# Sample cross-attention on four 32-column quarters of TensorE, two heads at a time

## What is computed

```
def cross_attend(h, mem_k, mem_v, w_q, w_o):          # 4 heads of 256, 256 memory tokens
    q = (h @ w_q).reshape(b, L, XA_HEADS, XA_HEAD_DIM)
    s = jnp.einsum('blhd,bmhd->bhlm', q, mem_k) * (XA_HEAD_DIM ** -0.5)
    p = jax.nn.softmax(s, axis=-1)
    o = jnp.einsum('bhlm,bmhd->blhd', p, mem_v).reshape(b, L, D_MODEL)
    return o @ w_o
```

## Time and profile before

| | |
|---|---|
| median of 3 runs | 1892.45 us (1890.16 to 1892.65) |
| the profiled execution, device time | 1889.55 us |
| its span, first to last instruction | 1887.5 us |
| TensorE busy in the span | 1793.5 us (95%) |
| VectorE / ScalarE / GpSimd busy | 506.8 / 300.8 / 31.9 us |
| read from memory | 356.67 MB, 202 GB/s over the span |

### The profile page before, as it was taken

How to read it: one execution, slowest core, us unless ns; L and a number is a source line. 1 busy time by engine, 2 the same in 40 slices (tenths; PEclk the granted TensorE clock), 3 DMA queues, 4 the chain that set the end, 5 groups by cost and what they waited for, 6 DMA issues and landing times.

```text
span 1887.5 us, 18695 instructions
## 1 busy us (share of the span) xinstructions
PE 1793.5 (95%) x7908; PEld 1127.3 (60%) x7908; DVE 506.8 (27%) x1066; ACT 300.8 (16%) x666; POOL 31.9 (2%) x34
## 2 busy tenths in 40 slices
PE   7999999999999899999899999999999998999996
PEld 5776676577666654444367666766667666544442
DVE  0027653441110311121200185534211013111122
ACT  2114220130120210001111142102211102100101
POOL 0000000000100000000000000000010000000000
PEclk9999999799999799999999999999999997999998
DMA  6323215553264279999813322255423551999992
GB/s 270 129 94 134 93 45 200 201 200 134 89 223 178 90 280 391 356 386 369 357 61 118 139 88 90 94 200 219 178 90 134 214 187 58 400 361 390 360 386 122
DMA packets 28681, 382.68 MB, mean 203 GB/s; under 512 B 3184, under 2 KB 3568, under 8 KB 3888
## 3 DMA queue, kind: packets, MB, share of 16 engines
q1 hardware_dynamic: 25040, 356.69, 48.9%
q0 software_dynamic: 3552, 24.71, 3.2%
HBM read 356.67 MB, written 24.71 MB: 202 GB/s over the span
## 4 chain that ended last, share of the span: by engine, by line
PE 87%; DVE 4%; ACT 4%; DVEq 2%; issue 1%; DMA 1%; ACTq 0%; POOL 0%; SPq 0%; POOLq 0%
PE psum L472 29%; PE psum L925 12%; PE psum L750 7%; PE psum L945 6%; PE psum L910 5%; PE psum L970 4%; PE psum L809 3%; PE psum L839 3%; PE psum L713 2%; PE psum L690 2%; PE psum L710 2%; DVE work L1455 2%; PE psum L700 2%; PE psum L479 1%; PE psum L877 1%
## 5 line engine op out<-in xcount | busy, mean ns | idle before, releaser
L472 PE MATMUL psum<-h,ring 128*128 128x320 f32 x1920 | 533.7, 438 | 7.7 <-DVE h L1380 6.3
L472 PEld LDWEIGHTS psum<-h,ring 128*128 128x128 f32 x1920 | 366.8, 192 | 164.9 <-issue 17.3
L925 PE MATMUL psum<-ring,work 128*64 128x512 f32 x1024 | 231.9, 597 | 1.6 <-ACT work L1325 1.4
L925 PEld LDWEIGHTS psum<-ring,work 128*64 128x64 f32 x1024 | 69.6, 137 | 137.3 <-issue 132.5
L750 PE MATMUL psum<-work,ring 128*128 128x320 f32 x512 | 138.3, 433 | 0.9 <-ACT work L1100 0.9
L472 PE MATMUL psum<-mem,ring 128*128 128x256 f32 x512 | 123.0, 395 | 4.0 <-ACT work L1100 4.0
L750 PEld LDWEIGHTS psum<-work,ring 128*128 128x128 f32 x512 | 97.1, 190 | 42.0 <-ACT work L1100 1.8
L945 PE MATMUL psum<-ring,work 128*64 128x512 f32 x512 | 115.1, 603 | 7.2 <-ACT work L1340 7.2
L472 PEld LDWEIGHTS psum<-mem,ring 128*128 128x128 f32 x512 | 98.5, 197 | 21.2 <-issue 7.1
L910 PEld LDWEIGHTS psum<-work 128*128 128x128 f32 x768 | 92.1, 199 | 25.0 <-issue 22.7
L910 PE MATMUL psum<-work 128*128 128x128 f32 x768 | 97.8, 286 | 1.4 <-ACT work L1313 1.4
(11 more groups left out here) (242 smaller groups left out, 1467.0 us busy)
## 6 DMA issues: line engine op xcount, KB each, us to landing
ring<-stream SPq DMA_DIRECT2D x168, 2048.0 KB, 9.1
st_out<-states_out POOLq DMA_DIRECT2D x18, 1024.0 KB, 9.2
mk_out<-k_mem POOLq DMA_DIRECT2D x2, 1024.0 KB, 6.1
mv_out<-work POOLq DMA_DIRECT2D x2, 1024.0 KB, 5.6
cst<-consts SPq DMA_DIRECT2D x1, 1456.0 KB, 22.3
x<-x_in SPq DMA_DIRECT2D x1, 1280.0 KB, 5.7
y_out<-h POOLq DMA_DIRECT2D x2, 640.0 KB, 3.2
mem<-mem_in SPq DMA_DIRECT2D x1, 1024.0 KB, 24.2
```

The costliest lines, as they stand in the source:

```text
L472: mm = pe.matmul(out, w[:, a:a + P], rhs[:, j, :], start=(j == 0), stop=(j == KD - 1))
L925: mm = pe.matmul(psum[ab * CAP:(ab + 1) * CAP, up, :], h_packed[:, p % 2, k, ab * CAP:(ab + 1) * CAP], w[:, a:a + BANK], start=(k == 0), s ...
```

## The change

The samples' matmuls use four quarters of the array, 32 columns each. In a group of four requests, request b has stationary columns of its own (its 8 tokens, no zeros), writes rows 32b to 32b+7 of PSUM, and four consecutive matmuls of the source go to four different quarters. The count stays at 64 matmuls for the scores and 64 for the outputs, each with 256 moving columns. `q_own`, `prob_own`, their zeroing on GpSimd and the waits for it are gone; the zero blocks' copies become plain ones (`q_all` takes a chunk in one copy).

Each sample group of four requests is now a tile of 128 rows with 32 used, so there are 4 tiles (`XT`: two of the prompt, two of samples) in place of 2 and a half, each processed for two heads at a time (`hp`). Transposes of probabilities: 32 per layer (24 before); of outputs: 16 (8 before). The transposed probabilities and transposed sample outputs leave PSUM by VectorE instead of ScalarE. Queries are computed in two halves, each followed by the scores of its two heads, and the quads are put in the order MQ0, K0, K1, MQ1, K2, K3, V0 to V3, MO0, MO1; a K or V quad holds four requests and two heads.

The layout constants, and then TensorE's list:

```diff
-Q_MQ = 24
-Q_KC, Q_VC = 26, 30
+Q_MQ = [24, 27]
+Q_KC, Q_VC = [25, 26, 28, 29], [30, 31, 32, 33]
+GB = DB // 4
+XT = 2 + GB
...
+                def queries(hp):
+                    for c in range(4 * hp, 4 * hp + 4):
+                        w = quad(pe, L, Q_MQ[hp])
+                        if c >= 4:
+                            pe.wait_ge(s_qout, L * KD + c - 3)
+                        products(psum[:, 4 + c % 4, 0:T], w, (c % 4) * SLAB, P, h,
+                                 L * NNORM + 1 if c == 0 else None).then_inc(s_q, 1)
+                    free(Q_MQ[hp])
+                def scores(hp):
+                    pe.wait_ge(s_qout, L * KD + 4 * hp + 4)
+                    for t in range(2):
...
+                    for gb in range(GB):
+                        q = Q_KC[2 * hp + gb]
+                        w = quad(pe, L, q)
+                        if hp == 1:
+                            pe.wait_ge(s_xexp, L * 8 + 2 + gb + 1)
+                        for rr in range(2):
+                            for c in range(2):
+                                k = 2 * (2 * hp + rr) + c
+                                for b in range(4):
+                                    own = SEQ + (4 * gb + b) * DS
+                                    a = ((b * 2 + rr) * 2 + c) * M
+                                    mm = pe.matmul(psum[32 * b:32 * b + DS, 2 + gb, rr * M:(rr + 1) * M],
+                                                   q_all[:, k, own:own + DS], w[:, a:a + M],
+                                                   start=(c == 0), stop=(c == 1))
+                                    if rr + c + b == 0:
+                                        first(mm)
+                        mm.then_inc(s_xs, 1)
+                        free(q)
+                def turn_probs(hp):
+                    for i in range(XT):
+                        u = 4 * hp + i
+                        pe.wait_ge(s_prob, L * 8 + u + 1)
+                        if hp == 0:
+                            pe.wait_ge(s_qout, L * KD + 4 + i + 1)
+                        else:
+                            pe.wait_ge(s_xoout, L * KD + i + 1)
+                        for rc in range(4):
...
+                def prompt_out(hp):
+                    for j in range(4 * hp, 4 * hp + 4):
+                        pe.wait_ge(s_ptout, L * 8 + 4 * hp + max(2, j % 4 + 1))
...
+                def sample_out(hp):
+                    pe.wait_ge(s_ptout, L * 8 + 4 * hp + 4)
+                    for gb in range(GB):
+                        q = Q_VC[2 * hp + gb]
+                        w = quad(pe, L, q)
+                        pe.wait_ge(s_xexp, L * 8 + 4 + 2 * hp + gb + 1)
+                        for rr in range(2):
+                            for c in range(2):
+                                for b in range(4):
+                                    own = SEQ + gb * P + 32 * b
+                                    a = ((b * 2 + c) * 2 + rr) * DV
+                                    mm = pe.matmul(psum[32 * b:32 * b + DS, 2 * hp + gb, rr * DV:(rr + 1) * DV],
+                                                   prob_t[:, 2 * hp + rr, c, own:own + DS], w[:, a:a + DV],
+                                                   start=(c == 0), stop=(c == 1))
+                                    if rr + c + b == 0:
+                                        first(mm)
+                        mm.then_inc(s_xos, 1)
+                        free(q)
+                def turn_out(hp):
+                    for gb in range(GB):
+                        pe.wait_ge(s_otok, L * 4 + 2 * hp + gb + 1)
+                        transposes([(psum[:, 2 * hp + gb, i * P:(i + 1) * P],
+                                     o_tok[:, gb, (4 * hp + i) * P:(4 * hp + i + 1) * P])
+                                    for i in range(4)]).then_inc(s_ott, 1)
+                queries(0)
+                scores(0)
+                queries(1)
+                scores(1)
+                turn_probs(0)
+                prompt_out(0)
+                sample_out(0)
+                turn_probs(1)
+                sample_out(1)
+                prompt_out(1)
+                turn_out(0)
+                turn_out(1)
+                pe.wait_ge(s_xoout, (L + 1) * KD)
+                pe.wait_ge(s_ottout, (L + 1) * 4)
```

ScalarE's order is queries(0), exps(0), queries(1), exps(1), prompt_out(0), sample_out(0), sample_out(1), prompt_out(1). VectorE's list, and what goes on GpSimd:

```diff
+                maxima(0)
+                probabilities(0)
+                maxima(1)
+                turned_probs(0)
+                probabilities(1)
+                turned_probs(1)
+                turned_out(0)
+                turned_out(1)
...
-                pool.wait_ge(s_wout, L * 16 + KD)
-                pool.memset(q_own[:], 0.0).then_inc(s_qzero, 1)
-                pool.wait_ge(s_mvstore, 16 * (L + 1))
-                pool.wait_ge(s_vt, (L + 1) * 4)
-                pool.memset(prob_own[:], 0.0).then_inc(s_pzero, 1)
```

More of the change, by code:

```diff
@@ L804, in attention @@
[L804 to L832, removed]
@@ L1259, in exps, with queries @@
[L1259 to L1266, removed]
+                def queries(hp):
+                    for c in range(4 * hp, 4 * hp + 4):
+                        act.wait_ge(s_q, L * KD + c + 1)
+                        act.activation(q_all[:, c, :], psum[:, 4 + c % 4, 0:T], ACT.Copy).then_inc(s_qout, 1)
@@ new lines, in prompt_out, with sample_out @@
+                def prompt_out(hp):
+                    for j in range(4 * hp, 4 * hp + 4):
+                        act.wait_ge(s_xo, L * KD + j + 1)
+                        act.activation(h[:, j, 0:SEQ], psum[:, 4 + j % 4, 0:SEQ], ACT.Copy).then_inc(s_xoout, 1)
+                def sample_out(hp):
+                    for gb in range(GB):
+                        act.wait_ge(s_xos, L * 4 + 2 * hp + gb + 1)
+                        act.activation(o_tok[:, gb, hp * BANK:(hp + 1) * BANK], psum[:, 2 * hp + gb, :], ACT.Copy)\
+                            .then_inc(s_otok, 1)
@@ L1708, in attention, with maxima @@
[L1708 to L1711 removed]
+                def maxima(hp):
+                    for i in range(XT):
+                        u = 4 * hp + i
+                        dve.wait_ge(s_xs, L * 8 + u + 1)
+                        dve.tensor_reduce(xmax[:, u, :], psum[:, i, :].rearrange("p (b m) -> p b m", b=2), AX.X, ALU.max)
+                        dve.drain()
+                        dve.tensor_scalar(xmax[:, u, :], xmax[:, u, :], -1.0 / 16, None, ALU.mult).then_inc(s_xmax, 1)
@@ new lines, in probabilities @@
+                def probabilities(hp):
+                    for i in range(XT):
+                        u = 4 * hp + i
+                        dve.wait_ge(s_xexp, L * 8 + u + 1)
+                        dve.reciprocal(xsum[:, u, :], xsum[:, u, :])
+                        dve.drain()
+                        pr = prob[:, i, 2 * hp:2 * hp + 2, :]
+                        dve.tensor_tensor(pr, pr, xsum[:, u, :].unsqueeze(2).broadcast_to([P, 2, M]), ALU.mult)\
+                            .then_inc(s_prob, 1)
```

167 lines of the change are left out of this document (58 added, 109 removed).

## The result

Median **1830.6 us** (4 runs, 1828.41 to 1838.72), before 1891.31 us beside it: ratio 0.9694, 95% interval 0.9656 to 0.9731, faster by 61 us where 71 were forecast. Later, beside another set of runs of the kernel before, the same kernel gave 0.9667 (0.9643 to 0.9690). Two executions further down, one of e5 (3089.9 us) and one of e6 (3520.7 us), were in a slow state that no edit explains, and all ratios and the medians of e5 and e6 leave them out.

The account below looks back on a forecast made before the run. TensorE, busy 95% of the span, was taken to bound the kernel. Cross-attention savings of 35.4 and 35.2 us, 70.6 in all, took 1889.55 to 1818.9; the median's 2.9 us offset gave 1821.8, range 1811 to 1845.

Parts of the forecast that it names:

- The mechanism: Sample matmuls: four quarters work through their own record lines side by side, 1.9 us a quad, 41 us a layer less before waits.
- the schedule: Hand timeline of one layer's cross-attention, from first query matmul to output projection: 78.0 us; 88.1 with two abreast, 116 with one.
- The 2.2 us a quad: Sample matmuls: a measured three-tile packing, 2.38 times, scaled to four as 3.2 times; sum some 3 us higher over both layers.
- One reading in the prediction: Sample matmuls, argument for the partly-abreast rival: eight records and eight loads must start in every 219 ns.
- the pitch of 55 ns: Sample matmuls: one record starting every 55 ns at the lower bound of 1.75 us a quad.
- the third, the waits: Cross-attention, part 3: new waits, worked out in a one-layer schedule; 35.4 and 35.2 us less per layer, 70.6 in all.
- VC3 late: Second sample outputs: the last V quad lands at about 69.7 us, so TensorE waits 2.1 us.
- The clock rival: Low clock after waits: 20 us of TensorE work up to twice as long, +10 to +15 us a layer, about 1845; chance 0.07.
- MQ1 late: Second half of the queries: the second query-weight quad lands at 27.3 us, so TensorE waits 0.5 us.
- the first four chunks: First half of the queries: with the copy of the fourth chunk, the scores start at 19.3 us.
- The pace behind one another: Quad loads: a lone quad lands 7.7 us after issue; behind another it takes 5.6 us more.
- VectorE's waits: Prompt and sample outputs: TensorE waits for VectorE's copies, 0.7 us before the first prompt outputs and 0.9 before later sample outputs.

Follow-up runs that it names:

- e5: Changed kernel with the first four query chunks in PSUM banks 0 to 3 and the prompt's V-copy wait behind the queries: 1831.3 us, ratio 0.9688.
- e6: Changed kernel with all 8 query chunks first, then the scores of both head pairs, quads reordered to match: 1826.2 us, ratio 0.9671.
- e1: Changed kernel with all sample matmuls on one quarter, leaving out three requests' outputs in four: 1896.0 us, ratio 1.0036 to the kernel before.
- e2: Changed kernel with requests alternating between two quarters, leaving out two requests' outputs in four: 1846.2 us, ratio 0.9763 to the kernel before.
- e4: Changed kernel with the last V quad, VC3, loaded early into a free part of the work area: 1810.8 us, ratio 0.9593.
- e8: Changed kernel with VC3 loaded into spare work area, MQ1 into the state-output buffer, and first query chunks in banks 0 to 3: 1809.3 us, ratio 0.9572.
- e11: The changed kernel as it is, measured and traced again beside the kernel before: 1829.0 us, ratio 0.9667.
- e7: Changed kernel with the request loop outermost, 8 records in a row on one quarter: 1846.8 us, ratio 0.9782 to the kernel before.
- e9: Changed kernel with the request loop between head and half, 4 records in a row on one quarter instead of 2: 1826.2 us, ratio 0.9644.
- e3: Changed kernel with the first output-weight quad, MO0, held back until the last V quad, VC3, has landed: 1831.1 us, ratio 0.9678.

## Why the prediction was right, and where it was off

- **The mechanism was right.** Quarters keep their own lines, four records run side by side, 1.75 to 1.8 us a quad against 1.9 forecast (bounds 1.75 and 2.15). e1 and e2 show that this is the whole gain, and that the schedule prices the other widths to 1 us. The 2.2 us a quad that the prediction estimated from a measured packing in the Trainium skill, TensorE: Matmul & The Clock Gate (Measured speedup vs the span model), did not come: one and four abreast are 13.98 and 3.64 us for two quads, 3.84 times. Three quarters alone, the case that the page measured, no run here shows. One reading in the prediction is wrong without harm: four records and four loads start in every 219 ns, not eight and eight; the pitch of 55 ns beside it is right.
- **The step that was mis-sized is the third, the waits.** The prediction had 78.0 us a window; they were 83.2 and 82.1. In layer 0 and 1: VC3 late by 4.8 and 3.1 us (forecast 2.1), and the 1.6 and 1.5 us that its pass then lost at the lower clock (forecast none, the clock was a rival at 0.07); MQ1 late by 1.1 and 2.1 (0.5); the first four chunks 1.4 and 1.0 us longer than in the schedule. That is 6.3 and 5.1 us; cheaper quads and transposes gave back about 1. Of these, e4 shows VC3 and its clock by removing them (7.1 and 5.7 us a window), e8 the rest. The pace behind one another was right in the mean (from VC0's landing to VC3's 18.5 and 15.7 us, forecast 16.7), but it scatters, and the queue began late: counted from the first query record, VC0 landed at 55.4 and 56.9 us where the schedule had 53.0, and VC3 at 73.9 and 72.6 where it had 69.7. In e11 the same terms are smaller in layer 0: a window of 80.6 us, VC3 late by 3.5.
- **A moved wait was overlooked.** The wait for the prompt's V copies stood behind the queries and now stands ahead of them, since the queries use the banks of the V transposes. The prediction has no term for it. It starts the queries 0.7 and 0.9 us later. Where the clock falls to 0.5 there, as it did in the trace of before, it is also low for more of their records, and the first four chunks take 20.1 to 20.7 us in place of 19.0 to 19.3; where it does not fall (layer 0 of e11), they take 18.0. e5 shows the earlier start and the shorter chunks, and also that putting the wait back alone gains nothing measurable.
- **The clock rival happened in small.** It fell in VC3's wait, for 3 us in one execution and 6 to 7 in another (e11, layer 0), and not for 25. The stretch of the earlier trace rows was no guide to how long it stays down.
- **VectorE's waits** were 0.35 and 1.26 us (forecast 0.7 and 0.9). GpSimd's zeroing, costed at nothing, brought nothing that can be seen: e1, also without it, has windows 2.9 and 3.2 us longer than before, where the schedule without such a gain had 2.7.
- **Not foreseen:** that putting the first scores ahead of the second queries is worth nothing by itself (e6). I had taken the order as given and had not asked what the other would give.

## What to carry to other kernels

Small matmuls with few stationary columns (8 here, 256 moving columns, float32) were cheapest when up to four records in a row went to one 32-row group of PSUM and the next to another; check in 10 ns windows how many records are under way. A fourfold faster step moves the question to the loads at once: write the landing of every transfer beside the step that needs it, and if one is late, look for room to load it earlier rather than for a better order. A wait that a change only moves is an edit as well. And before a difference of a few microseconds is explained, trace the same kernel twice.

## What the runs showed of the hardware that I had not expected

- A quarter works ahead of program order: with 8 records in a row on one quarter, the next quarter's first record starts together with the fifth of them, before three that stand ahead of it (e7). With 4 in a row the width is full (e9, 3.66 us for two quads).
- Records with their weight loads can be fed every 56 ns: 64 of them in 3.57 us, from 536.67 to the next group's start at 540.24. The 67 ns of the 64 x 64 transposes was no limit.
- After TensorE was busy 1.91 of 4 us and then 0.24 of 4 us, the granted clock was 0.50; 3 us of full work later it was at 0.99 again, in e11 6 to 7 us later. The same program may or may not see it fall: ahead of layer 0's queries, with the same work, it was 0.50 in one execution of the changed kernel and 1.00 in another, and the four chunks took 20.7 and 18.0 us.
- A 2 MB transfer behind another landed 5.2 us after it at one time and 7.0 at another, at the same place of the program (VC3 behind VC2 in layers 1 and 0 of the changed kernel; 5.5 and 7.0 in layers 0 and 1 of e3). Why is open.
